# Two query-weight pieces kept on the chip, six row buffers up to step 112, and an early second row

## What is computed

```python
q = (xt @ w_query).reshape(T, PEER_HEADS, 2, PEER_KEY_DIM // 2)     # 8 heads
s = jnp.einsum('thcd,hckd->thck', q, sub_keys)
s_top, i_top = lax.top_k(s, PEER_TOPK)                              # 16 of 128, twice
cand = (s_top[:, :, 0, :, None] + s_top[:, :, 1, None, :]).reshape(...)
cand_idx = (i_top[:, :, 0, :, None] * PEER_KEYS + i_top[:, :, 1, None, :]).reshape(...)
g_s, g_pos = lax.top_k(cand, PEER_TOPK)                             # 16 of 256 sums
e_idx = jnp.take_along_axis(cand_idx, g_pos, axis=-1)
g = jax.nn.softmax(g_s, -1)
h = gelu(einsum('td,thkd->thk', xb, expert_u[e_idx]))               # one row of u per expert
y = einsum('thk,thkd->td', g * h, expert_v[e_idx])                  # one row of v per expert
```

## Time and profile before

| | |
|---|---|
| median of 3 runs | 940.52 us (939.14 to 941.0) |
| profiled execution | 939.81 us, its span 937.9 us |
| PE busy | 757.0 us, 81% of the span |
| DVE, ACT, POOL busy | 64%, 46%, 32% |
| DMA | 339.54 MB, mean 362 GB/s; rows alone 268.45 MB |
| granted TensorE clock, mean | 0.82 |

### The profile page before, as it was taken

The page is one execution under the profiler, slowest core; times in us unless marked ns, Lnnn a source line. Parts: engine busy times, 40 slices in busy tenths (PEclk is TensorE's granted clock), DMA queues, the critical chain, the costliest instruction groups (busy, mean ns, idle before and its releaser), DMA issues.

```text
span 937.9 us, 11751 instructions
## 1 busy us (share of the span) xinstructions
PE 757.0 (81%) x4032; PEld 347.8 (37%) x4032; DVE 599.6 (64%) x1437; ACT 430.8 (46%) x1184; POOL 299.6 (32%) x295
## 2 busy tenths in 40 slices
PE   8999999999879989889675787777766777676664
PEld 6886665655624544443121433232311111111110
DVE  1622853546698969686657565786667666677445
ACT  1143315422579888764334434364443434434333
POOL 0010031002334536434233334343533334333430
PEclk9999999999968979989796857687967656566676
DMA  7634555548999999999999999999999999999993
GB/s 272 257 122 172 226 199 194 223 180 313 424 422 388 423 420 418 423 419 422 424 423 420 422 419 423 420 420 423 421 419 421 421 421 421 421 420 422 419 421 143
DMA packets 46140, 339.54 MB, mean 362 GB/s; under 512 B 6112, under 2 KB 6144, under 8 KB 9216
## 3 DMA queue, kind: packets, MB, share of 16 engines
q0 software_dynamic: 37152, 268.45, 69.2%
q1 hardware_dynamic: 8928, 70.34, 19.1%
HBM read 337.70 MB, written 1.06 MB: 361 GB/s over the span
## 4 chain that ended last, share of the span: by engine, by line
DMA 46%; PE 35%; ACT 8%; DVE 7%; issue 3%; POOL 1%; DVEq 0%; SPq 0%; ACTq 0%; POOLq 0%
DMA late<-in_uv,eidx 30%; DMA ring<-in_uv,eidx 15%; PE ps L721 6%; PE ps L1129 6%; PE ps L745 6%; PE ps L912 4%; PE ps L869 4%; ACT late L1178 4%; ACT L1178 3%; DVE late L1930 2%; DVE ring L1930 2%; PE ps L728 1%; PE ps L737 1%; ACT tmp L1178 1%; PE ps L809 1%
## 5 line engine op out<-in xcount | busy, mean ns | idle before, releaser
L1178 ACT ACTIVATE late<-late 128x1 f32<-128x1 f32 (+3 forms) x787 | 222.1, 285 | 330.3 <-DVE late L1930 312.0
L1129 PE MATMUL ps<-ring,late 64*64 64x512 f32 x928 | 167.5, 810 | 76.9 <-ACT late L1178 76.7
L1129 PE MATMUL ps<-late 64*64 64x512 f32 x960 | 164.9, 783 | 73.3 <-ACT late L1178 73.0
L2029 POOL DMA_INDIRECT late<-in_uv,eidx x118 | 128.9, 1093 | 233.9 <-PE ps L1129 173.7
L1930 DVE CUSTOM_DVE_ANT_0 late<-late,x_sb 128x1024 f32<-128x1024 f32 x120 | 146.9, 1225 | 84.1 <-DMA late<-in_uv,eidx 83.7
L1930 DVE CUSTOM_DVE_ANT_0 ring<-ring,x_sb 128x1024 f32<-128x1024 f32 x116 | 142.1, 1225 | 85.7 <-DMA ring<-in_uv,eidx 85.0
L2029 POOL DMA_INDIRECT ring<-in_uv,eidx x116 | 126.6, 1091 | 192.9 <-PE ps L1129 181.4
L1178 ACT ACT_TABLE_LOAD x85 | 109.1, 1283 | 27.2 <-PE ps L737 14.6
L1129 PEld LDWEIGHTS ps<-late 64*64 64x64 f32 x960 | 31.9, 158 | 181.8 <-ACT late L1178 163.9
L1129 PEld LDWEIGHTS ps<-ring,late 64*64 64x64 f32 x928 | 30.3, 160 | 178.4 <-ACT late L1178 164.5
L1178 ACT ACTIVATE tmp<-ps 128x512 f32<-128x512 f32 (+4 forms) x79 | 38.8, 499 | 65.0 <-PE ps L721 41.2
(11 more groups left out here) (267 smaller groups left out, 769.7 us busy)
## 6 DMA issues: line engine op xcount, KB each, us to landing
wring<-in_wts SPq DMA_DIRECT2D x21, 2048.0 KB, 11.6
ring<-in_wts SPq DMA_DIRECT2D x2, 2048.0 KB, 8.8
wring<-in_wts SPq DMA_DIRECT2D x2, 1428.0 KB, 5.8
wring<-in_wts SPq DMA_DIRECT2D x2, 1388.0 KB, 6.3
ring<-decay_sums SPq DMA_DIRECT2D x2, 1024.0 KB, 5.8
lnw<-in_ln SPq DMA_DIRECT2D x4, 512.0 KB, 12.2
late<-in_uv,eidx POOLq DMA_INDIRECT x118, 16.9
ring<-in_uv,eidx POOLq DMA_INDIRECT x116, 16.9
```

The costliest lines, as they stand in the source:

```text
L1129: last = mm(o[t][n * HD:(n + 1) * HD, :], factor[tokens, :], values[tokens, n * 512:(n + 1) * 512], start=start, stop=stop, skip_group_che ...
L1178: return nc.scalar.activation(out, in_, func, **kw)
L2029: G.indirect_dma_start(row(slots[g]), None, uv, bass.IndirectOffsetOnAxis(eidx[:, u % 2, k:k + 1], 0)).then_inc(row_here[slots[g]], 16)
```

## The change

Four things are changed.

1. **Two weight pieces less.** For i = 1 the query groups are taken in the order of the pieces 3, 2, 0, 1. Piece q3, loaded for i = 0, stays in its half of `wring` until i = 1 has used it (`kept`); piece q2 is loaded once, into `ring3`, behind the gate product that held it (`wq_here`), and serves both tiles. The heads of i = 1 are therefore worked in the order 6, 7, 4, 5, 0, 1, 2, 3.
2. **Six row buffers.** As `ring3` holds weights, rows go round over six buffers up to step 112 (KEEP_ROWS); then the two in `ring3` join, once PE has finished query group 1 of i = 1 (`q`, 1, 1), and from 160 on it is ten as before. Rows 4 and 5 now lie in `ring2` and wait for z 0 rather than z 1.
3. **Weights of w_out for i = 1 in one half.** Since q3 holds the other half, w_out 0 to 3 of i = 1 follow each other in the same half of `wring`; `homes` and `piece_behind` tell where a piece goes and what it waits for. The table moves the mixer product's parts: 61, 63, 68, 70, 77, 78, 84, 86 instead of 64, 67, 69, 71, 77, 79, 81, 83, with the transposes ahead of them at 57 instead of 60, and the query groups of i = 1 start at 95 and 103 (before 94 and 108).
4. **Row 1 early.** The second best expert is one of two pairs. GpSimd forms both sums and both numbers, DVE compares the sums, and GpSimd picks the number (`second_expert`), so that row 1 no longer waits for the choice of eight.

```diff
-QUERIES = [[(0, 0, 1), (0, 1, 1), (1, 0, 2), (2, 0, 1), (2, 1, 1), (3, 0, 1), (3, 1, 1)], [(n, 0, 2) for n in range(4)]]
+QUERIES = [[(0, 0, 1), (0, 1, 1), (1, 0, 2), (2, 0, 1), (2, 1, 1), (3, 0, 1), (3, 1, 1)], [(n, 0, 2) for n in (3, 2, 0, 1)]]
+KEPT = 3
-SLOT_ORDER = [0, 1, 2, 3, 6, 7, 4, 5]
+KEEP_ROWS = 112
...
-    queries(1, 0, 94, 2, 3)
-    queries(1, 1, 108, 4, 4)
+    queries(1, 0, 95, 2, 3)
+    queries(1, 1, 103, 4, 4)
...
-        slots = [SLOT_ORDER[g % RING0] if g < SWITCH else (g - SWITCH + RING0) % RING for g in range(NT * STEPS)]
+        slots = [g % 6 if g < KEEP_ROWS else (g - KEEP_ROWS + 6) % RING0 if g < SWITCH else (g - SWITCH + RING0) % RING for g in range(NT * STEPS)]
...
+        kept_at = len(pieces) - 2 - 4 - 1
+        homes = [n % WSLOTS for n in range(kept_at + 1)]
+        homes += [1 - homes[kept_at]] * 5 + [homes[kept_at]]
+        loads = [sum(homes[n] == homes[m] for n in range(1, m + 1)) for m in range(len(pieces))]
+        def piece_behind(k):
+            return max(n for n in range(k) if homes[n] == homes[k])
...
                 if k == 18:
                     await_full(sp, "qT", 1, 3)
                     sp.dma_start(ring2[:, :], wts[:, starts[10]:starts[11]]).then_inc(wz0_here, 16)
+                    await_full(sp, "z", 1, 1)
+                    sp.dma_start(ring3[:, :], wts[:, starts[20]:starts[21]]).then_inc(wq_here, 16)
...
-                    end = pieces[k - WSLOTS][2]
+                    end = pieces[piece_behind(k)][2]
...
+                    if piece == 2:
+                        pe.wait_ge(wq_here, 16)
+                        query[0] = ring3[:, :].rearrange("p (k n) -> p k n", k=KD)
+                    elif (i, piece) == (1, KEPT):
+                        query[0] = kept[0]
...
+                dve.wait_ge(rivals_ready, 1)
+                tt(ahead, rivals[:, 0:1], rivals[:, 1:2], ALU.is_ge).then_inc(ahead_ready, 1)
...
+            def second_expert():
+                link(G.tensor_scalar(scaled, leaders[:, 0, :], float(NKEY), None, ALU.mult))
+                for n in range(2):
+                    last = G.tensor_tensor(experts_of[:, n:n + 1], scaled[:, n:n + 1], leaders[:, 1, 1 - n:2 - n], ALU.add)
+                link(last)
+                link(G.tensor_tensor(apart_by, experts_of[:, 0:1], experts_of[:, 1:2], ALU.subtract))
+                pool.wait_ge(ahead_ready, 1)
+                link(G.tensor_tensor(apart_by, apart_by, ahead, ALU.mult))
+                link(G.tensor_tensor(apart_by, apart_by, experts_of[:, 1:2], ALU.add))
+                link(G.tensor_copy(eidx[:, 0, 1:2], apart_by))
...
-                elif g in (1, TOPK // 2):
-                    pool.wait_ge(idx_ready, 2 + (g > 1))
+                elif g in (2, TOPK // 2):
+                    pool.wait_ge(idx_ready, 2 + (g > 2))
                 if g == 4:
-                    await_full(pool, "z", 1, 1)
-                if g == 6:
                     await_full(pool, "z", 0, 1)
+                if g == KEEP_ROWS:
+                    await_full(pool, "q", 1, 1)
```

64 lines of the change are left out of this document (42 added, 22 removed).

## The result

The changed kernel takes **947.46 us** (median; 942.35 to 954.10), the kernel before 939.83 us beside it. The ratio is 1.0086, with a 95% interval from 1.0065 to 1.0107. Forecast was 938.0 with a range from 931 to 946, so the time lies outside it, on the slow side. The profiled execution takes 946.17 us, its span 944.3; it is 6.4 us above the profiled execution of before. The executions also spread more: 12 us where before has 4.6.

A forecast was written before the change was run, and what follows sets the result against it. The prediction took DMA bytes as the bound: -10.0 us (two pieces less), -1.4 (q2 early), +2.9 and +3.7 (six buffers), +2.3 (wait at row 112), 0 (w_out) make -2.5, so 938.0 us, range 931 to 946.

The follow-up runs named there:

- after_busy24: The changed kernel with two rounds of products of zeros on TensorE just ahead of row 24; 945.0 us, 1.0071 of the kernel before.
- after_paired: The changed kernel with the exponentials of two heads of the second tile's attention in one ScalarE step; 949.49 us, 1.0105 of the kernel before.
- kept3_second: The changed kernel with eight row buffers again and only q3 kept, q2 loaded twice as before; 933.03 us, 0.9925 of the kernel before.
- ring6: The kernel before with six row buffers up to step 112, no weight piece kept; 957.97 us, 1.0201 of the kernel before.
- kept3_second_paired: kept3_second with the exponentials of two heads of the second tile's attention in one ScalarE step; 935.46 us, 0.9959 of the kernel before.

## What to carry to other kernels

- What a ring of buffers must cover is the longest round of one buffer: from a row's landing through each engine's queue to the next issue, and on to the next landing. Count it at the busiest stretch and divide by the spacing of the stream. Here 13.4 + 5.5 us is over seven rows of 2.49 us, and six buffers can't cover it. The flat 422 GB/s in the trace with eight buffers did not tell that one buffer less would cost 5.4 us.
- Take a shallower ring's loss as a feedback (late rows slow the engines, and slow engines make the next rows late), not as a sum of places: from eight to seven to six buffers it went 0, 5.4, 17.7 us. A mended place shows the next one (after_busy24, after_paired).
- Of a bundle of edits, the free ones should be timed alone: one kept piece and the early row with eight buffers give 933.0 us, clearly apart from the kernel before, and no version was clearly faster.

## What the runs showed of the hardware

- TensorE's granted clock fell to 1.2 GHz at 317.0 in the kernel after, 1.1 us after a halt of 2.88 us had ended, and rose at 327.2, with TensorE busy for all of the time between. In kept3_second it was low from 338.0 to 351.6, behind a halt of 3.15 us that ends at 338.0; in ring6 from 314.8 to 321.7, behind one of 2.88, and from 342.2 to 359.2, behind one of 2.57. In the kernel before it was low from 337.7 to 347.9, around two halts of 1.6 and 1.7 us, but with eight buffers the rate stays at 422 there. After the halt of 2.59 us that ends at 372.58 in the kernel after it stayed at 2.4 GHz. With products of zeros in the halt before row 24 it stayed there too, until 341.
- 30 table loads of ScalarE, 38.5 us, cost nothing with eight buffers (939.39 us without, 939.27 with) and 14.3 us with six.
- In the full stream of the kernel before, the 16 DMA engines drift apart, from 1.9 us between the first and the last to finish a row to 8.8 us at the end. In the kernel after, with its pauses, it is 5.0 us at the end, and 2.1 of its 8.5 us of loss come back there.
- The 16 executions of the kernel after lie within 12 us, those of before within 4.6, those of kept3_second_paired (10) within 9 and those of ring6 (4) within 3.4. What makes them spread is not shown.
